# A convolution stage with all 31 taps on TensorE, in groups of 32 output columns

## The reference

```python
def conformer_conv(h, w_pw1, b_pw1, w_dw, b_dw, ln_g, ln_b, w_pw2, b_pw2):
    a = h @ w_pw1 + b_pw1
    u = a[..., :D_MODEL] * jax.nn.sigmoid(a[..., D_MODEL:])
    u = lax.conv_general_dilated(u, w_dw[:, None, :].astype(u.dtype), window_strides=(1,),
                                 padding=[(CONV_WIDTH - 1, 0)],
                                 dimension_numbers=('NWC', 'WIO', 'NWC'),
                                 feature_group_count=D_MODEL) + b_dw
    uf = u.astype(jnp.float32)
    mu = jnp.mean(uf, axis=-1, keepdims=True)
    var = jnp.mean(jnp.square(uf - mu), axis=-1, keepdims=True)
    u = ((uf - mu) * lax.rsqrt(var + EPS) * ln_g + ln_b).astype(h.dtype)
    return jax.nn.silu(u) @ w_pw2 + b_pw2
```

## Time and profile before

| | before |
|---|---|
| time, median of 3 runs | 2484.92 us (2484.28 to 2485.14) |
| profiled execution: its time / its span | 2485.75 us / 2483.9 us |
| busy: PE, DVE, ACT, POOL | 94%, 55%, 35%, 11% |
| mean granted clock of TensorE | 0.976 |
| stage from the second tile of `T_PW1` (662.4 us) to the first matmul of `T_PW2` (900.3 us) | 237.9 us |
| the same stage: PE, DVE, ACT, POOL busy | 153.6, 214.6, 92.4, 128.2 us |

### The profile page before, as it was taken

How to read it: one execution, slowest core, us unless ns; L and a number is a source line. 1 busy time by engine, 2 the same in 40 slices (tenths; PEclk the granted TensorE clock), 3 DMA queues, 4 the chain that set the end, 5 groups by cost and what they waited for, 6 DMA issues and landing times.

```text
span 2483.9 us, 29402 instructions
## 1 busy us (share of the span) xinstructions
PE 2336.0 (94%) x10367; PEld 1864.3 (75%) x10367; DVE 1376.2 (55%) x1657; ACT 867.2 (35%) x1172; POOL 278.7 (11%) x231
## 2 busy tenths in 40 slices
PE   8988999999966679999999998999999999999997
PEld 7866788888744348888888776788888788788886
DVE  4443443434699965444354785745544754744553
ACT  4266432322533444323233454422222322422221
POOL 0011100000365611000011331000001001000001
PEclk9999999999987889999999999999999999999999
DMA  5211233333311103333333111233333233233331
GB/s 183 77 43 34 77 95 100 93 102 93 102 34 43 42 17 110 97 94 98 98 105 102 60 51 41 87 102 94 97 97 94 84 101 93 80 99 94 101 93 51
DMA packets 58131, 208.55 MB, mean 84 GB/s; under 512 B 6449, under 2 KB 6594, under 8 KB 57922
## 3 DMA queue, kind: packets, MB, share of 16 engines
q1 hardware_dynamic: 58050, 207.42, 27.7%
HBM read 205.30 MB, written 2.10 MB: 83 GB/s over the span
## 4 chain that ended last, share of the span: by engine, by line
PE 58%; DVE 4%; ACT 2%; issue 1%; POOL 0%; ACTq 0%; DVEq 0%
PE ps L1358 55%; DVE wlo L718 1%; ACT whi L308 1%; PE ps L1811 1%; PE ps L1785 1%; PE ps L1744 0%; PE ps L1801 0%; PE ps L1790 0%; DVE cv L1007 0%; ACT sq L317 0%; PE ps L1818 0%; DVE m L749 0%; DVE m L1171 0%; DVE h L921 0%; DVE odd L1007 0%
## 5 line engine op out<-in xcount | busy, mean ns | idle before, releaser
L1358 PE MATMUL ps<-xh,whi 128*128 128x512 f32 x1764 | 699.9, 397 | 8.0 <-DVE wlo L718 5.8
L1358 PE MATMUL ps<-xh,wlo 128*128 128x512 f32 x1764 | 687.5, 390 | 0.0
L1358 PE MATMUL ps<-xl,whi 128*128 128x512 f32 x1764 | 687.3, 390 | 0.0
L718 DVE TENSOR_TENSOR wlo<-raw,whi 128x1024 fp32r<-128x1024 f32 x380 | 483.6, 1273 | 259.3 <-ACT whi L308 247.7
L308 ACT ACTIVATE whi<-raw 128x1024 fp32r<-128x1024 f32 x380 | 398.3, 1050 | 457.5 <-PE ps L1358 456.7
L1358 PE MATMUL ps<-yh,whi 128*128 128x512 f32 x1117 | 438.0, 392 | 1.4 <-DVE yl L889 1.4
L1358 PE MATMUL ps<-yl,whi 128*128 128x512 f32 x1117 | 435.4, 390 | 0.0
L1358 PE MATMUL ps<-yh,wlo 128*128 128x512 f32 x1117 | 435.3, 390 | 0.0
L1358 PEld LDWEIGHTS ps<-xh,whi 128*128 128x128 f32 x1764 | 332.0, 188 | 87.4 <-issue 9.0
L1358 PEld LDWEIGHTS ps<-xl,whi 128*128 128x128 f32 x1764 | 332.0, 188 | 72.0 <-issue 4.8
L1358 PEld LDWEIGHTS ps<-xh,wlo 128*128 128x128 f32 x1764 | 331.5, 188 | 69.9
(11 more groups left out here) (225 smaller groups left out, 2154.2 us busy)
## 6 DMA issues: line engine op xcount, KB each, us to landing
raw<-stream SPq DMA_DIRECT2D x384, 512.0 KB, 3.6
h<-x_t SPq DMA_DIRECT2D x8, 256.0 KB, 7.6
out_t<-h SPq DMA_DIRECT2D x8, 256.0 KB, 2.0
const<-consts SPq DMA_DIRECT2D x1, 1089.0 KB, 11.1
wgr<-w_glr SPq DMA_DIRECT2D x1, 512.0 KB, 8.1
vec<-vecs SPq DMA_DIRECT2D x1, 212.0 KB, 2.6
wg<-w_gate SPq DMA_DIRECT2D x1, 17.0 KB
```

The source lines that it names most:

```text
L718: dve.tensor_tensor(wlo[:, a.slot], raw[:, a.slot], whi[:, a.slot].bitcast(F32), ALU.subtract)\
L1358: mm = pe.matmul(out, lhs, rhs, start=first and n == 0, stop=last and n == 2)
```

## The change

Per channel block, none of the 31 taps is left on VectorE, ScalarE or GpSimd. The gated block in `ub` (now 128x542 with its padding) is copied by 16 SBUF-to-SBUF transfers into `u4`: channel group i (32 channels) goes, shifted by d = 0 to 3 tokens, to partitions 32d to 32d+31 of `u4[:, b % 3, i]`. A matmul then contracts over 128 partitions, which are 4 shifts x 32 channels, with a 128x32 weight block of `tapw`; 8 of them, at offsets 0, 4, ... 28, make 32 taps (the last has weight zero). The four channel groups write four different column groups of 32 partitions of the same PSUM bank. `tapw` (4.2 MB) is a new input, laid out on the host; it lies where `yh` and `yl` lie later. For the norm, a pivot (minus the mean of blocks 0 and 1) is subtracted from each block as it comes, and sums of the centred values and of their squares run along on VectorE; at the end the remaining mean is taken off again. The loops of the stage are written out.

```diff
-TAPS_PE = 6
-TAPS_POOL = 10
+SHIFTS = 4
+TAP_GROUPS = 8
+TAPS_PE = SHIFTS * TAP_GROUPS
+COPY = T + SHIFTS * (TAP_GROUPS - 1)
+PIVOT = 2
+CENTERED = 5
...
+            def spread(b):
+                arrived = s(f"u4_in{b % 3}")
+                sp.wait_ge(s("pw_u"), b + 1)
+                if b >= 3:
+                    sp.wait_ge(s("cv_pe"), 4 * (b - 2))
+                for d in range(SHIFTS):
+                    for i in range(4):
+                        sp.dma_start(A["u4"][32 * d:32 * d + 32, b % 3, i], A["ub"][32 * i:32 * i + 32, b % 2, d:d + COPY])\
+                          .then_inc(arrived, 16)
...
+            sp.wait_ge(tile_done, T_PW1)
+            sp.dma_start(tapw[:], taps.rearrange("p (b i m c) -> p b i m c", b=KB, i=SHIFTS, m=TAP_GROUPS))\
+              .then_inc(s("taps_in"), 16)
+            for b in range(KB):
+                n = T_PW1 + 8 + 2 * b
+                load(n // RING, n % RING)
+                load(n // RING, n % RING + 1)
+                spread(b)
...
+            for b in range(KB):
+                take_value(b)
+                if b >= 3:
+                    take_conv(b - 3)
+                if b == 4:
+                    pivot_sum()
+                if b == 5:
+                    pivot()
+                take_gate(b)
+                gated(b)
...
-                for k in range(TAPS_PE):
-                    mm = pe.matmul(ps[:, 5 + u], A["dg"][:, u, k], A["ub"][:, u, k:k + T], start=k == 0,
-                                   stop=k == TAPS_PE - 1)
...
+                pe.wait_ge(s(f"u4_in{b % 3}"), 16 * SHIFTS * 4 * (b // 3 + 1))
+                if b >= 2 + CENTERED:
+                    pe.wait_ge(s("cen_ready"), b - 1)
+                elif b >= 2:
+                    pe.wait_ge(s("cv_done"), b - 1)
+                for m in range(TAP_GROUPS):
+                    for i in range(4):
+                        mm = pe.matmul(ps[32 * i:32 * i + 32, 5 + b % 2], tapw[:, b, i, m],
+                                       A["u4"][:, b % 3, i, SHIFTS * m:SHIFTS * m + T], start=m == 0,
+                                       stop=m == TAP_GROUPS - 1)
...
+            for n in range(1, 2 * KB):
+                tile(Tile(T_PW1 + n), n % RING, xh, xl)
+                if n == 9:
+                    pe.wait_ge(s("piv_sum"), 1)
+                    pe.matmul(ps[:, 7], cst("ones"), A["s1"][:], start=True, stop=True).then_inc(s("piv_mm"), 1)
+                if n >= 5 and n % 2:
+                    conv((n - 5) // 2)
+            conv(6)
+            conv(7)
...
-            first_round(Tile(T_PW2), FIRST, yh, yl, yh_ready, y_ready, Y0["pw"])
-            for j in range(FIRST, KB):
+            keep_clock(15, 5)
+            first_round(Tile(T_PW2), RING, yh, yl, yh_ready, y_ready, Y0["pw"], None, 1)
+            for j in range(RING, KB):
```

More of the change, by code:

```diff
@@ L100, in loaded, with build @@
         return self.rounds * 16 + 16 * (self.n // RING + 1)
-def build(nc, x_t, stream, w_glr, w_gate, vecs, consts, out_t):
+def build(nc, x_t, stream, w_glr, w_gate, vecs, consts, taps, out_t):
     with ExitStack() as ctx:
@@ L541, in _, with cen_square @@
             inv_rms("pw", D)
[L542 to L563, removed]
+            act.preload_act_table_set("sigmoid_and_others")
+            def cen_square(k):
                 act.wait_ge(s("cen_ready"), k + 1)
                 if k >= 2:
-                    act.wait_ge(s("var_mm"), k - 1)
+                    act.wait_ge(s("ln_acc"), max(k - 2, 1))
                 else:
@@ L971, in _ @@
             dve.memset(A["ub"][:, :, 0:PAD], 0.0).then_inc(s("pw_zero"), 1)
+            dve.memset(A["ub"][:, :, PAD + T:], 0.0).then_inc(s("pw_zero"), 1)
             dve.wait_ge(rrow_ready, SUM["pw"] + 1)
[L973 to L989 removed]
@@ L1038, in _, with take_value @@
-            dve.wait_ge(s("mu_copied"), 1)
-            for k in range(KB):
-                dve.tensor_tensor(A["cv"][:, k], A["cv"][:, k], A["mu"][:], ALU.subtract).then_inc(s("cen_ready"), 1)
-            dve.wait_ge(rrow_ready, SUM["lnvar"] + 1)
+            def take_value(b):
+                t = Tile(T_PW1 + 2 * b)
+                dve.wait_ge(tile_done, t.count)
+                dve.tensor_tensor(ps[:, t.slot], ps[:, t.slot], rrow[:], ALU.mult).then_inc(s("pw_t1"), 1)
+                split_lo(t)
@@ new lines, in _ @@
+            for b in range(KB):
+                take_value(b)
[7 more added lines that the diff above has]
+                gated(b)
+                if b == 5:
+                    center(0)
+                    center(1)
+                    sum_values(1)
+                if b == 6:
+                    center(2)
+                    sum_cen_squares(1)
+                    center(3)
+                    sum_values(2)
+                    sum_values(3)
+                if b == 7:
+                    center(4)
+                    sum_cen_squares(2)
+                    sum_values(4)
+                    sum_cen_squares(3)
@@ L1996, in _vectors, with _taps @@
     return f
+def _taps(a):
+    w = np.concatenate([a["cv_w_dw"][0], np.zeros((TAPS_PE - TAPS, D), a["cv_w_dw"].dtype)]).reshape(TAP_GROUPS, SHIFTS, KB, SHIFTS, 32)
+    f = np.zeros((SHIFTS, 32, KB, SHIFTS, TAP_GROUPS, 32), w.dtype)
+    for c in range(32):
+        f[:, c, :, :, :, c] = w[:, :, :, :, c].transpose(1, 2, 3, 0)
+    return f.reshape(P, KB * TAPW)
 def _constants():
@@ L2041 @@
         "consts": _constants(),
+        "taps": _taps(a),
     }
```

249 lines of the change are left out of this document (130 added, 119 removed).

## The result

The changed kernel takes 2402.11 us in the median of 4 runs (2401.7 to 2405.05), against 2484.6 us before: a ratio of 0.9672, with a 95% interval of 0.9656 to 0.9689. The forecast was 2396, so 6 us of the 88.6 forecast did not come. The profiled execution took 2402.08 us and is 83.67 us shorter than the one of before.

The account below looks back on a forecast made before the run. VectorE was taken to bound the convolution stage: 2485.75 us, minus 90.4 for the earlier start of the second projection, plus 1.0 given back there, makes 2396.4, so 2396 us. The range was 2388 to 2420, holding 0.82.

Parts of the forecast that it names:

- The bound: Convolution stage: VectorE, busy 25.88 of 27 us, holds up TensorE; work put on TensorE costs nothing until 27.3 us a block.
- Four column groups at once: Convolution taps: four column groups run at the same time, so a block's 32 matmuls take 6.83 us, not 27.3.
- Rivals 1, 2 and 4: Taps per block: two streams at a time, 13.65 us, chance 0.11; packs waiting to drain, 9.4, 0.08; no overlap, 27.3, 0.03.
- The estimate by the Trainium skill of 8.9 us a block: Convolution taps: 27.3 us divided by the skill's 3.07x for four row groups; 16 us more in all.
- The sum for the stage: Convolution stage: 15 tiles 81.6, taps 54.6, pivot matmul 0.85, changes 1.2, together 138.3 us, ending at 800.8 us.
- the changes between whole array and column groups: Convolution stage: 12 switches of TensorE's mode at 0.1 us each, 1.2 us, bounds 0 to 0.3 each.
- The tail: From the last taps to the second projection: sums, variance, logarithm, exponential and on, 9.1 us; projection starts 90.4 us earlier.
- The second projection: Its start: 17.9 us from first matmul to first h instead of 16.9, so 1.0 us is given back.
- the +1.0 for four tiles in place of three: Start of the second projection: 17.9 us to first h with four tiles at once, against 16.9 before.
- The transfers: Shifted copies of the gated block: 0.38 us each to issue, 16 take 6.1 us; no wait taken, last block tight.
- rival 5: Last block's transfers late by 4 to 15 us, TensorE idle and at half clock after: 2400 to 2416, chance 0.06.
- Rival 3: Shifted copies land one after another at 2.0 us, 16 take 32 us a block: slower, 2530 us, chance 0.04.

Follow-up runs that it names:

- the two other orders: The changed kernel with a block's 32 matmuls reordered: column groups in pairs, 2435.85 us, or one group after the other, 2515.88 us.

## Why the prediction was right, and where it was off

- **The bound.** Right: VectorE's order held up TensorE. The two kernels with VectorE's load put back sharpen it: in the changed kernel the 15 taps alone cost 2.9 us, and with GpSimd's additions in six blocks 38.5. In the kernel before it is the multiply-adds beside GpSimd's additions that raise the means from 0.74 to 1.15 and 1.35 us. The prediction named ScalarE too; it had no products in these kernels, and it stands idle beside slow multiply-adds of the kernel before. So the load that mattered for a period was the pair of VectorE and GpSimd. The kernel before without GpSimd's additions was not run, so how much of its 27.3 us they alone explain is not measured.
- **Four column groups at once.** Right: 6.83 us forecast, 6.91 to 6.94 measured where blocks follow each other. Rivals 1, 2 and 4 (13.65, 9.4 and 27.3 us a block) fell by the loads in fours; the two other orders show that it is the order of issue that gives them their work at once. The estimate by the Trainium skill of 8.9 us a block (TensorE: Matmul & The Clock Gate, Measured speedup vs the span model) is not what this stream shows.
- **The sum for the stage.** 138.3 us from the first tile to the last tap, 143.9 measured (660.56 to 804.45): 2.62 of wait, 1.8 of low clock in block 7, and 1.2 that is the changes between whole array and column groups. These I took at 0.1 each. A period measures 18.10 us against 17.71 of tiles and taps, so 0.39 for two changes, 0.2 each, inside the bounds of 0 to 0.3. That it goes by changes and not by blocks is seen where blocks follow each other: one takes 7.00 us, two 13.87, three 20.74, so each further block adds 6.87.
- **The tail.** 9.1 forecast, 9.12 measured. That it is worth its place was tested: 10.7 us with the old one.
- **The second projection.** 17.9 us to the first h forecast, 19.6 measured, and 17.8 where the fill reaches up to it (809.69 to 827.46). So the work was sized right and the clock was not: the prediction had the fill over in time and costing nothing, and took the clock behind it as full. It ends 2 us too early, and in this execution the clock fell behind that stop. And the +1.0 for four tiles in place of three was too small: at full clock it is 2.45. The 16.9 us of before were no clean price of three tiles, since its first matmuls were 0.43 us apart and not 0.23, at half clock.
- **The transfers: the term that was mis-sized.** The prediction had SyncE issue a copy every 0.38 us, from the 0.333 us of its weight loads, 6.1 us for 16. It is 0.591 and the gap between, 0.634 us, and with one of 1.45 us among them the 16 take 10.88 us. The place was the one named (rival 5, the last block alone): forecast landing 12.3 to 13.5 us after the tile's end, measured 16.5 (779.19 to 795.68), against 13.87 of cover. "Each further microsecond costs one" was too little too: 2.62 us of wait brought 1.8 us of low clock with it. With both, this is 4.4 of the 7.7 us by which the terms were exceeded (below), and the kernel with two issuing engines gives back 4.0 in the median.
- **Rival 3** (transfers one after another, slower) fell: a copy lands 2.6 us after its issue in the median, and the next is issued after 0.63 us already. The 2.0 us that the prediction cites beside this rival from the Trainium skill (DMA: Bandwidth & Descriptors, Anatomy of one DMA) are given there for transfers that GpSimd issues. SyncE issues these; the fastest of them land in 2.0 us too.

The terms add up: 5.6 in the stage, 1.7 at the projection's start and 0.4 behind its evictions (36.3 us from the first h to full speed, not 35.9: the two sum matmuls ahead of the full-speed tiles take 1.56 us, and 1.12 in the kernel before) are 7.7 us more than forecast. The 2.1 us ahead of the stage go the other way. They have nothing to do with the change, so it is luck that the total is off by less than its terms.

Not settled: why the clock near 256 us differs from execution to execution. Its 1 to 3 us are in every comparison of single traces here, which is why stretches inside the stage were compared. Why a stop of 2.06 us is followed by a fall of the clock in some executions and not in others is open too.

## What to carry to other kernels

The price of a transfer's issue has to be taken from a transfer of the same kind: here 0.59 us for a copy between parts of SBUF on 32 partitions and 0.33 us for a weight load of 512 KB. The copy's price stayed the same with half its bytes. Many small copies in a row ahead of a wait want two issuing engines, or to stand ahead of what is not urgent. Before work is moved off a slow VectorE, look at GpSimd beside it: in the changed kernel the same 15 operations a block cost 2.9 us alone and 38.5 with its additions beside them. And a wait of 2 to 3 us ahead of TensorE costs 1.7 to 1.8 times its length where the clock falls behind it (2.62 us brought 1.8 more, 2.07 us 1.7 more); a wait of 0.45 us did not bring that, nor did one of 2.06 us in another kernel.

## What was not expected of the hardware

- Column groups that get their work one after the other still overlap at the borders, by 3.6 to 3.9 steps of 0.429 us: 12.18 and 22.52 us a block in place of 13.7 and 27.5.
- SyncE's issue of a copy of 32 partitions takes 591 ns for 2160 bytes a row and for 1080 alike.
- VectorE's multiply-add of 128x512 takes 745 ns alone and 1.52 us beside GpSimd's additions, which themselves take 1.48 us in the median; in the kernel before it takes 1.78 us beside them.
